# Another distance between the matmul operands in SBUF: normalised tiles at a pitch of 528 words, weight slots 32 bytes apart within 512

## What is computed

```python
for layer in range(DEPTH):                    # 2 layers
    h = rms_norm(x, norm_mix[layer])
    m = mixer_a(...) if layer == 0 else mixer_b(...)
    x = x + m                                 # each mixer ends in out @ w_out (1024 x 1024)
    x = x + conv_ffn(rms_norm(x, norm_ffn[layer]), ...)

def conv_ffn(h, w_up, conv_w, conv_b, w_down):
    u = h @ w_up                              # 1024 x 5632
    u = conv_b + sum(conv_w[j] * up[:, j:j + S] for j in range(3))
    gate, val = jnp.split(u, 2, axis=-1)
    return (jax.nn.silu(gate) * val) @ w_down # 2816 x 1024
```

## Time and profile before

| | before |
|---|---|
| median of 3 runs | 1269.09 us (1268.56 to 1269.21) |
| the profiled execution, its own time | 1270.43 us |
| its span in the trace | 1268.6 us |
| TensorE matmul busy | 1230.6 us, 97% |
| VectorE busy | 767.5 us, 60% |
| ScalarE busy | 547.5 us, 43% |
| GpSimd busy | 212.5 us, 17% |
| share of the 16 DMA engines' time in use by the main queue | 25.9% |

### The profile page before, as it was taken

The page is one execution under the profiler, slowest core; times in us unless marked ns, Lnnn a source line. Parts: engine busy times, 40 slices in busy tenths (PEclk is TensorE's granted clock), DMA queues, the critical chain, the costliest instruction groups (busy, mean ns, idle before and its releaser), DMA issues.

```text
span 1268.6 us, 17242 instructions
## 1 busy us (share of the span) xinstructions
PE 1230.6 (97%) x6080; PEld 980.8 (77%) x6080; DVE 767.5 (60%) x1337; ACT 547.5 (43%) x933; POOL 212.5 (17%) x262
## 2 busy tenths in 40 slices
PE   7999999999999999999999878999999999999999
PEld 4868886677788888878887766777788888887887
DVE  3577895754766666563327778762775666664334
ACT  5554435653633333342225676652543433343221
POOL 3314243430400000000003672430400000000000
PEclk9999999999999999999999998999999999999999
DMA  6422222203222232213232110013322222212323
GB/s 231 164 100 78 92 67 67 75 27 133 100 100 99 86 106 73 103 46 102 96 99 94 61 35 1 1 34 97 108 95 99 99 99 99 88 61 83 99 90 108
DMA packets 25120, 110.83 MB, mean 87 GB/s; under 512 B 2752, under 2 KB 3136, under 8 KB 17776
## 3 DMA queue, kind: packets, MB, share of 16 engines
q1 hardware_dynamic: 25072, 110.21, 25.9%
HBM read 108.06 MB, written 6.33 MB: 90 GB/s over the span
## 4 chain that ended last, share of the span: by engine, by line
PE 87%; DVE 6%; POOL 2%; issue 2%; ACT 2%; DMA 1%; SPq 0%; DVEq 0%; ACTq 0%; POOLq 0%
PE ps L1719 25%; PE ps L1720 24%; PE ps L1721 24%; PE ps L1480 3%; PE ps L1499 3%; PE ps L1380 2%; PE ps L1368 2%; DVE h_lo L947 1%; DVE xT L1143 1%; PE ps L1463 1%; DVE w_lo L941 1%; PE ps L1363 1%; PE ps L1453 1%; PE ps L1691 1%; POOL rope_tmp L483 1%
## 5 line engine op out<-in xcount | busy, mean ns | idle before, releaser
L941 DVE TENSOR_TENSOR w_lo<-raw,w_hi 128x1024 fp32r<-128x1024 f32 (+4 forms) x114 | 194.7, 1708 | 258.4 <-ACT w_hi L575 258.4
L1719 PE MATMUL ps<-h_hi,w_hi 128*128 128x512 f32 (+1 forms) x712 | 279.3, 392 | 2.0 <-DVE w_lo L941 2.0
L1720 PE MATMUL ps<-h_lo,w_hi 128*128 128x512 f32 (+1 forms) x712 | 279.4, 392 | 0.0
L575 ACT ACTIVATE w_hi<-raw 128x1024 fp32r<-128x1024 f32 (+4 forms) x124 | 177.7, 1433 | 234.0 <-PE ps L1721 233.8
L1721 PE MATMUL ps<-h_hi,w_lo 128*128 128x512 f32 (+1 forms) x712 | 277.5, 390 | 0.0
L1719 PE MATMUL ps<-a_hi,w_hi 128*128 128x512 f32 x480 | 189.5, 395 | 1.9 <-DVE w_lo L941 1.5
L1720 PE MATMUL ps<-a_lo,w_hi 128*128 128x512 f32 x480 | 188.7, 393 | 0.0
L1721 PE MATMUL ps<-a_hi,w_lo 128*128 128x512 f32 x480 | 188.7, 393 | 0.0
L1719 PEld LDWEIGHTS ps<-h_hi,w_hi 128*128 128x128 f32 (+1 forms) x712 | 133.6, 188 | 33.1 <-DVE w_lo L941 2.9
L1721 PEld LDWEIGHTS ps<-h_hi,w_lo 128*128 128x128 f32 (+1 forms) x712 | 133.6, 188 | 29.5 <-issue 0.6
L1720 PEld LDWEIGHTS ps<-h_lo,w_hi 128*128 128x128 f32 (+1 forms) x712 | 133.7, 188 | 27.8 <-issue 0.5
(11 more groups left out here) (189 smaller groups left out, 1528.5 us busy)
## 6 DMA issues: line engine op xcount, KB each, us to landing
raw<-in_f_up SPq DMA_DIRECT2D x44, 1024.0 KB, 4.8
raw<-in_f_w_down SPq DMA_DIRECT2D x44, 512.0 KB, 3.4
raw<-in_a_in_wide SPq DMA_DIRECT2D x13, 1024.0 KB, 4.9
bias_tiles<-bias_rows SPq DMA_DIRECT2D x1, 4096.0 KB, 19.5
raw<-in_a_w_out SPq DMA_DIRECT2D x8, 512.0 KB, 3.4
raw<-in_b_w_out SPq DMA_DIRECT2D x8, 512.0 KB, 3.4
xT<-in_xt SPq DMA_DIRECT2D x4, 512.0 KB, 6.0
toep_b<-bias_tiles SPq DMA_DIRECT2D x8, 256.0 KB, 2.7
```

The costliest lines, as they stand in the source:

```text
L575: sc.activation(w_hi[:, s, 0:n], raw[:, s, 0:n], ACT.Copy).then_inc(w_hi_done, 1)
L941: dve.tensor_tensor(w_lo[:, s, 0:n], raw[:, s, 0:n], w_hi[:, s, 0:n].bitcast(F32), ALU.subtract)\
L1719: pe.matmul(dst, s_hi, m_hi, start=start, stop=False)
L1720: pe.matmul(dst, s_hi, m_lo, start=False, stop=False)
```

## The change

Three things are moved, and no instruction is added or removed:

- the pitch of the two slots of `raw`, `w_hi` and `w_lo` goes from 2064 to 2056 words, so that slot 1 lies at 32 instead of 64. The pads behind each tensor grow by the 16 words that it lost, so that all slots 0 stay where they were;
- the pitch of the 8 tiles of `h_hi` and `h_lo` goes from 512 to 528 words. Tile k then lies at 64 (k + 1), modulo 512, instead of at 64. The buffers that share the space are spread over the longer region by 128 more words in the middle and 128 at the end;
- `pad_a` grows by 4 words, which the rounding of starts makes 32 bytes, behind a region that grew by 1024 bytes. Both slots of `a_hi` and `a_lo` then lie at 32 instead of 0 (141856 bytes behind the start of `w_hi`, 277 x 512 + 32).

```diff
-SLOT_PITCH = SLOT + 16
+SLOT_PITCH = SLOT + 8
+H_PITCH = S + 16
...
         raw = sb("raw", [P, 2, SLOT_PITCH])
-        sb("pad_raw", [P, 96])
+        sb("pad_raw", [P, 112])
         w_hi = sb("w_hi", [P, 2, SLOT_PITCH], F32R)
-        sb("pad_w_hi", [P, 96])
+        sb("pad_w_hi", [P, 112])
         w_lo = sb("w_lo", [P, 2, SLOT_PITCH], F32R)
-        sb("pad_w_lo", [P, 96])
+        sb("pad_w_lo", [P, 112])
...
-            h_hi = sb("h_hi", [P, KD, S], F32R, scope)
-            h_lo = sb("h_lo", [P, KD, S], F32R, scope)
+            h_hi = sb("h_hi", [P, KD, H_PITCH], F32R, scope)
+            h_lo = sb("h_lo", [P, KD, H_PITCH], F32R, scope)
...
-        sb("pad_h0", [P, S])
+        sb("pad_h0", [P, S + 128])
...
+        sb("pad_h1", [P, 128])
...
-        sb("pad_a", [P, 112])
+        sb("pad_a", [P, 116])
...
-                sc.activation(h_hi[:, k, :], xT[:, k, :], ACT.Identity,
+                sc.activation(h_hi[:, k, 0:S], xT[:, k, :], ACT.Identity,
...
-                        ins = product3(pe, ps[:, 4 + q, :], w_hi[:, s, cols], w_lo[:, s, cols], h_hi[:, k, :],
-                                       h_lo[:, k, :], k == 0, k == KD - 1)
+                        ins = product3(pe, ps[:, 4 + q, :], w_hi[:, s, cols], w_lo[:, s, cols], h_hi[:, k, 0:S],
+                                       h_lo[:, k, 0:S], k == 0, k == KD - 1)
```

More of the change, by code:

```diff
@@ L256, in hybrid_layers_kernel @@
         diag = sb("diag", [P, T, P])
-        sb("pad_q", [P, 16 * S - (112 + 4 * S + 4 * (S + 4) + 4 * S + 2 * S)])
+        sb("pad_q", [P, 16 * S - (116 + 4 * S + 4 * (S + 4) + 4 * S + 2 * S)])
         ps = ctx.enter_context(nc.psum_tensor("ps", [P, 8, 512], F32))
@@ L946, in prepare_lo @@
                 dve.wait_ge(hi_ok[n], ORDER[n].index(k) + 1)
-                dve.scalar_tensor_tensor(h_lo[:, k, :], xT[:, k, :], gain[:, gain_at + k:gain_at + k + 1],
-                                         h_hi[:, k, :].bitcast(F32), ALU.mult, ALU.subtract)\
+                dve.scalar_tensor_tensor(h_lo[:, k, 0:S], xT[:, k, :], gain[:, gain_at + k:gain_at + k + 1],
+                                         h_hi[:, k, 0:S].bitcast(F32), ALU.mult, ALU.subtract)\
                     .then_inc(lo_ok[n], 1)
@@ L1348, in _ @@
                 ins = product3(pe, ps[0:A_SMALL, 7, :], w_hi[:, k // 4, cols], w_lo[:, k // 4, cols],
-                               h_hi[:, k, :], h_lo[:, k, :], k == 0, k == KD - 1)
+                               h_hi[:, k, 0:S], h_lo[:, k, 0:S], k == 0, k == KD - 1)
                 if k == 3:
@@ L1587, in feed_forward @@
                         cols = slice((2 * k + q) * P, (2 * k + q + 1) * P)
-                        ins = product3(pe, ps[:, 4 + q, :], w_hi[:, 0, cols], w_lo[:, 0, cols], h_hi[:, k, :],
-                                       h_lo[:, k, :], j == 0, j == KD - 1)
+                        ins = product3(pe, ps[:, 4 + q, :], w_hi[:, 0, cols], w_lo[:, 0, cols], h_hi[:, k, 0:S],
+                                       h_lo[:, k, 0:S], j == 0, j == KD - 1)
                         if j == KD - 1:
```

## The result

The changed kernel takes 1278.95 us (median of 3 runs, 1278.14 to 1279.66) against 1269.09 us: 1.0079 times the time of before, 95% interval 1.0056 to 1.0101. It is slower by 9.9 us, and 2 us above the top of the predicted range (1277). The span of the profiled execution went from 1268.6 to 1277.2 us, by 8.6 us.

A forecast was written before the change was run, and what follows sets the result against it. TensorE's matmul pace was taken as the bound, set by d, moving minus stationary operand's place in bytes modulo 512. Terms -4.6 + 5.6 + 0.4 = +1.4 us on 1269.1 gave 1270.5 us, range 1264.5 to 1277.

The forecast's parts named there:

- 10.0 us of excess over d = 0: FFN up 2.4, onto the residual 5.4, projection A 2.2 us: the most any choice of addresses could win back.
- Onto the residual: Matmuls with a moving: slot 1 at d = 0 wins 5.4 us, slot 0 at +32 costs 0.8; net -4.6 us.
- the price of +32: Slot 0 onto the residual: taken as 1.1 ns per matmul, half the price of d = +64; 0.8 us.
- FFN up: Matmuls with h moving: distances spread over sixteen values cost 8.0 us against 2.4 now, +5.6 us.
- the price of a spread: FFN up and projection A: distances changing with every triple taken to cost 3.8 ns per matmul.
- The two stretches with a spread: Projection B's second half, 3.1 ns per matmul over the cheapest, and the small first projection, 5.4 ns.
- a sign of being wrong: Prediction fails if price goes by something finer than d, such as order of distances or a stretch's inherited pace.
- Projection A and the rest: Projection A: 2.6 us of excess against 2.2, +0.4; projection B, small first projection and latents taken as 0.
- The rival "slower", in its harsher form: +32 priced like -64 onto the residual and 6.6 ns in FFN up's slot 1: 1277.5 us; chance 0.06.
- The rival that the addresses don't matter: Whole kernel: pace differs by slot for another reason, time stays at 1269.1 us; chance 0.03.

The follow-up runs named there:

- the sums moved: Eight matmuls summing the first norm's squares moved 12 matmuls later: 1258.97 us against the all-distances-zero kernel; 1268.77 us against the kernel before.
- m3: Against the kernel before, other places only: slot 1 at 16, h at 0, a at 32 bytes; 1267.16 us in one run.
- m4: Against the kernel before, other places only: slot 1 and h at 256, a at 0 bytes; 1261.6 us in one run.
- m2: Against the kernel before, other places only: slot 1 at 192, a at 160, h at 192 bytes; 1278.65 us in one run.

## Why the prediction was wrong

*What bounds the kernel.* Right: TensorE's pace is the kernel's time, the pace goes by d, and the other engines stayed hidden. The prediction had counted out 10.0 us of excess over d = 0; with all distances at zero and the sums moved in both kernels, 9.8 us went.

*Onto the residual: the term that failed most.* It was put at -4.6 us and came to -0.9. Its first half was right: slot 1 at d = 0 fell to 227 ns. The failed step is the price of +32: "Between d = 0 (0 ns) and d = +64 (2.2 ns) I take the half, 1.1 ns". Measured, it is 6.3 ns, more than at +64. The distance was taken as something along which a price rises evenly; the map shows it going 0, 6.4, 2.3, 6.7 in steps of 32. The bound given beside it, 6.6 ns and a net of -0.6, is nearly what was measured.

*FFN up.* It was put at +5.6 us and came to +8.0: 4.9 ns per matmul against 3.8, so the price of a spread was put 1.1 ns too low. The two stretches with a spread, 3.1 and 5.4 ns, did enclose the value; the nearer one was the small first projection, to which I gave the smaller weight for its 72 columns. The sum also took a spread to cost one price wherever it stands; the triples show that it depends on the order of distances, which the prediction had named as a sign of being wrong. The runs show in addition that slots and pitch each take slot 1 of FFN up away from d = 0, and that either one alone would have cost about the same.

*Projection A and the rest.* Its slot 0 went from 233.2 to 231.8 ns and the steps read of its slot 1 from 227 to 233, less and more as expected. Together with all the parts that were put at 0 (projection B, the small first projection, the latents) it came to 1.5 us, against 0.4; which of them took the 1.1 us is not shown.

*The sum.* -0.9 + 8.0 + 1.5 = 8.6 us of span, where the prediction had +1.4: 3.7 us of the miss lie onto the residual, 2.4 in FFN up and 1.1 in the rest. The rival "slower", in its harsher form with +32 priced like -64, had -0.6 and +8.6 and ended at 1277.5 us; it comes near what happened and was given 0.06. The range ended half a microsecond below its time and had no room for scatter above it. The rival that the addresses don't matter fell with every run.

*The two read ports.* The Trainium skill ("SBUF — State Buffer", section "Who interferes with whom") says that TensorE's two read ports, for the moving operand and for LDWEIGHTS, are independent, and that TensorE never waits on anyone. By that rule nothing would have changed. The runs disagree: up to 7 ns in 227 by the distance between the two operands alone. The same page gives SBUF cachelines of 16 bytes ("Specifications (TRN2)"). Here a distance of 16 bytes costs at most 0.4 ns and one of 32 costs 6.3 (m3); no run shows what unit is behind that.

*What stays open.* Why the price has this shape, with 64 cheaper than 32 and 96, was not settled; nor was which of the two reads is held up. That the loads of the next stationary operand are the partner of the moving read is still an inference, from the fact that only the distance matters (the kernel before, the zero-distance kernel, m3 and m4 have these operands at different places, and all take 10.88 us for 48 matmuls at a distance of 0) and that the two overlap in the trace.

## What to carry to other kernels

Where float32r matmuls of 512 columns with a fresh stationary operand fill TensorE, let the moving and the stationary operand start at the same place modulo 256 bytes, in every slot and tile: here that was worth 10 us of 1269 in the matmuls, for a few pads. Other widths and types have to be measured anew. Don't interpolate between measured offsets; measure the very offset. And when TensorE gets faster, look where it now waits longer: with a gap of two microseconds at the start, and the half clock behind it, 4 of the 10 us were missing until other matmuls were put into it.

## What the runs showed of the hardware

- A back-to-back float32r matmul of 512 columns with its own weight load takes 226.7 ns when its operands lie 0 or 256 bytes apart modulo 512 (zero distances, m4), and 228.9 to 234 ns at the distances of 32 to 224 bytes modulo 256 that were tried, with the clock at 1.00.
- The price is not monotone: 0, 6.4, 2.3, 6.7, 5.7, 7, 6.7 and 7 ns in steps of 32 bytes.
- It depends on what went before: in m2, behind a stretch at 192, the 48 matmuls at d = 0 take 10.91 instead of 10.88 us.
- The clock fell to the 1.2 GHz level after TensorE had stood still for 2.24 us at 28 to 31 us, and stayed at 1.00 when it did not stand still. The length of the gap alone did not decide it: with the slots alone a gap of 1.33 us was followed by a mean of 0.76 between 31 and 38 us, while the kernel before had 1.36 us and m3 had 1.61 us, and both kept 1.00 there.
